# Band attention in a two-layer encoder: softmax weights of seven head pairs turned by VectorE and a DRAM round trip

## What is computed

```python
sc = jnp.einsum('bqhd,bkhd->bhqk', qc, kc).astype(jnp.float32) * scale + bias[None]
sc = jnp.where(valid[None, None, None, :], sc, NEG_INF)
p = jax.nn.softmax(sc, axis=-1).astype(vc.dtype)
return jnp.einsum('bhqk,bkhd->bqhd', p, vc)
```

## Time and profile before

| | |
|---|---|
| median of 3 runs | 1094.41 us (1094.17 to 1094.53) |
| profiled execution, own time | 1094.57 us |
| its span in the trace | 1092.8 us |
| mean granted clock of TensorE | 0.999 of full speed |
| TensorE matmul busy | 1085.8 us |
| VectorE, ScalarE, GpSimd busy | 642.3, 469.5, 521.3 us |
| DMA | 106 GB/s over the span |

### The profile page before, as it was taken

How to read it: one execution, slowest core, us unless ns; L and a number is a source line. 1 busy time by engine, 2 the same in 40 slices (tenths; PEclk the granted TensorE clock), 3 DMA queues, 4 the chain that set the end, 5 groups by cost and what they waited for, 6 DMA issues and landing times.

```text
span 1092.8 us, 15012 instructions
## 1 busy us (share of the span) xinstructions
PE 1085.8 (99%) x5040; PEld 902.6 (83%) x5040; DVE 642.3 (59%) x1081; ACT 469.5 (43%) x698; POOL 521.3 (48%) x408
## 2 busy tenths in 40 slices
PE   9999999999999999999999999999999999999998
PEld 7888888888888888888888888888888888888886
DVE  6586557766666642223488777766777676751103
ACT  7874443433333333323555555564443333333213
POOL 6578635544444545554433333344544444445541
PEclk9999999999999999999999999999999999999999
DMA  9382323222222233333322222222322222224312
GB/s 307 98 261 97 116 78 111 101 96 96 96 96 96 97 101 111 110 101 115 116 87 89 97 81 97 75 77 78 116 96 96 96 96 96 96 97 139 114 36 77
DMA packets 44726, 115.63 MB, mean 106 GB/s; under 512 B 11376, under 2 KB 13552, under 8 KB 44688
## 3 DMA queue, kind: packets, MB, share of 16 engines
q1 hardware_dynamic: 42224, 110.65, 30.7%
q10 hardware_dynamic: 2464, 4.47, 1.3%
HBM read 111.92 MB, written 6.59 MB: 108 GB/s over the span
## 4 chain that ended last, share of the span: by engine, by line
PE 99%; DMA 0%; ACT 0%; DVE 0%; SPq 0%; issue 0%; DVEq 0%; ACTq 0%
PE bank L1493 29%; PE bank L1495 29%; PE bank L1494 28%; PE bank L1580 2%; PE bank L1781 2%; PE bank L1778 2%; PE bank L1780 2%; PE bank L1955 2%; PE bank L1940 2%; PE bank L1970 1%; PE bank L1969 1%; DMA x<-x_in 0%; PE bank L1756 0%; PE bank L1755 0%; DVE rows_out L1466 0%; ACT xh L567 0%
## 5 line engine op out<-in xcount | busy, mean ns | idle before, releaser
L472 POOL TENSOR_TENSOR wl<-raw,wh 128x512 fp32r<-128x512 f32 x187 | 244.7, 1309 | 540.9 <-ACT wh L563 540.9
L563 ACT ACTIVATE wh<-raw 128x1024 fp32r<-128x1024 f32 x187 | 197.7, 1059 | 354.7 <-PE bank L1495 284.0
L1493 PE MATMUL bank<-xh,wh 128*128 128x512 f32 x880 | 344.5, 392 | 0.0
L1495 PE MATMUL bank<-xh,wl 128*128 128x512 f32 x880 | 342.9, 390 | 0.0
L1494 PE MATMUL bank<-xl,wh 128*128 128x512 f32 x880 | 342.8, 390 | 0.0
L474 POOL TENSOR_TENSOR wl<-raw,wh 128x512 fp32r<-128x512 f32 x187 | 253.8, 1357 | 0.0
L1493 PEld LDWEIGHTS bank<-xh,wh 128*128 128x128 f32 x880 | 165.3, 188 | 34.5
L1495 PEld LDWEIGHTS bank<-xh,wl 128*128 128x128 f32 x880 | 165.2, 188 | 34.5
L1494 PEld LDWEIGHTS bank<-xl,wh 128*128 128x128 f32 x880 | 165.4, 188 | 33.6
L1494 PE MATMUL bank<-al,wh 128*128 128x512 f32 x252 | 98.1, 389 | 0.0
L1493 PE MATMUL bank<-ah,wh 128*128 128x512 f32 x252 | 98.1, 389 | 0.0
(11 more groups left out here) (245 smaller groups left out, 1480.5 us busy)
## 6 DMA issues: line engine op xcount, KB each, us to landing
raw<-weights SPq DMA_DIRECT2D x187, 512.0 KB, 3.3
bias_scratch<-ext_scratch SPq DMA_DIRECT2D x1, 4096.0 KB, 17.9
bias<-bias_scratch ACTq DMA_DIRECT2D x8, 512.0 KB, 3.5
raw<-weights SPq DMA_DIRECT2D x8, 256.0 KB, 7.3
x<-x_in SPq DMA_DIRECT2D x8, 256.0 KB, 7.0
out<-rows_out SPq DMA_DIRECT2D x4, 256.0 KB, 2.0
x_rows<-blocks SPq DMA_DIRECT2D x16, 48.0 KB, 2.6
out<-x SPq DMA_DIRECT2D x3, 256.0 KB, 2.6
```

What stands on the lines that cost most here:

```text
L472: nc.gpsimd.tensor_tensor(low[:, 0:FIRST], raw[:, c % RAW, 0:FIRST], high[:, 0:FIRST], ALU.subtract).then_inc(w_half, 1)
L563: nc.scalar.activation(wh[:, c % RING].rearrange("p k c -> p (k c)"), raw[:, c % RAW], ACT.Copy).then_inc(w_hi, 1)
L1493: nc.tensor.matmul(dst, w_hi_part, m_hi, start=first, stop=False)
L1495: return nc.tensor.matmul(dst, w_lo_part, m_hi, start=False, stop=last)
```

## The change

P of the pairs 0 to 6 is no longer turned by TensorE. ScalarE normalises P in place (`normalise` moved from VectorE); VectorE turns each of the ten 128 x 128 blocks of a head within its 32 x 32 blocks (`turn_p`, 20 instructions a pair) into `p_blocks`; SyncE stores each head's 640 KB to a DRAM scratch `p_scratch` (of shape 2 x 128 x 1280) and, when that has landed, loads it back with four DMAs of 32 partitions each, which bring the 32 x 32 blocks to their places, into `pt`. `pt` shares its memory with `ptl`, `p_blocks1` with `p_sb`. ScalarE writes the high part from `pt`, two instructions a head, GpSimd the low part. `weighted_v(c - 1)` runs in pair c: inside K of the next pair, and in the pairs 4 and 5 behind it. It reads P and writes PSUM in pieces of 32 columns. The low part of Q moves from VectorE to GpSimd. The first part of Q of the pair after takes five of eight steps, not four. The output halves of the first pairs' result move one pair back, so that pair 4 has none, and two more fall into the last pair. Pair 7 still turns P on TensorE (`transpose_p`, `weighted_v_last`), between other products. Banks, waits, unit numbers and the packing order of the weights follow; SyncE's loop over the weight units is written out around the attention, since the stores and loads of P stand between its loads. Below is the diff's core, with the indentation cut.

```diff
-Q_AHEAD = KT // 2
+Q_AHEAD = 5
+AV_AFTER_K = (4, 5)
 EARLY = PAIRS // 2
...
+TURNED_AT = [0, 4, 7, 9]
+QUARTER = P_COLS // 4
+FIRST_UNROLLED, LAST_UNROLLED = 15 * RAW, 22 * RAW
...
+ptl_at = nc.sbuf_base
 ptl = att_mem("ptl", [P, 2, P_COLS], F32R)
+pt = nc.alloc_sbuf_tensor_at("pt", [P, 2, P_COLS], F32, offset=ptl_at)
...
+p_blocks = [att_mem("p_blocks0", [P, 4, QUARTER], F32),
+            nc.alloc_sbuf_tensor_at("p_blocks1", [P, 4, QUARTER], F32, offset=p_sb_at)]
...
+def first_unit(c):
+    return U_PAIR + 3 * c - (c > EARLY)
+def split_unit(c):
+    return U_PAIR + 3 * c + 3 - (c > EARLY)
...
+def store_blocks(c, hh):
+    sp.wait_ge(p_turned, 10 * (2 * c + hh) + 10)
+    sp.wait_ge(p_in[hh], 64 * c)
+    sp.dma_start(p_d[hh], p_blocks[hh][:].rearrange("p b n -> p (b n)")).then_inc(p_stored[hh], 16)
+def load_turned(c, hh):
+    sp.wait_ge(p_stored[hh], 16 * c + 16)
+    sp.wait_ge(av_mm, 2 * c)
+    for b in range(4):
+        sp.dma_start(pt[32 * b:32 * b + 32, hh].rearrange("p (a n) -> p a n", a=4),
+                     bass.AP(p_d.tensor, hh * P * P_COLS + b * QUARTER,
+                             [[P_COLS, 32], [32 * P_COLS, 4], [1, QUARTER]])).then_inc(p_in[hh], 16)
+with sp.Fori(0, FIRST_UNROLLED // RAW - 3) as turn:
+    for c in range(3 * RAW, 4 * RAW):
+        load_unit(c, turn)
+n = FIRST_UNROLLED
+for c in range(PAIRS - 1):
+    while n < first_unit(c + 1) + RAW:
+        load_unit(n)
+        n += 1
+    store_blocks(c, 0)
+    store_blocks(c, 1)
+    load_turned(c, 0)
+    load_turned(c, 1)
+for c in range(n, LAST_UNROLLED):
...
+def p_split_lo(c, hh):
+    for n in range(2):
+        pool.wait_ge(p_hi, 4 * c + 2 * hh + n + 1)
+        at = slice(2 * QUARTER * n, 2 * QUARTER * n + 2 * QUARTER)
+        nc.gpsimd.tensor_tensor(ptl[:, hh, at], pt[:, hh, at], pth[:, hh, at], ALU.subtract).then_inc(p_lo, 1)
+def q_split_lo(c):
+    pool.wait_ge(qk_hi, 2 * c + 1)
+    nc.gpsimd.tensor_tensor(ql[:], q_sb[:], qh[:], ALU.subtract).then_inc(ql_pool, 1)
+for c in range(FIRST_UNROLLED, U_PAIR + 3):
+    split_lo(c)
+for c in range(PAIRS - 1):
+    unit = split_unit(c)
+    q_split_lo(c + 1)
+    split_lo(unit)
+    split_lo(unit + 1)
+    p_split_lo(c, 0)
+    if c != EARLY and c != PAIRS - 2:
+        split_lo(unit + 2)
...
+def normalise(c, hh):
+    act.wait_ge(rsum_inv, 2 * c + hh + 1)
+    for h, i in SCORE_STEPS:
+        if h == hh:
+            blk = p_sb[:, hh, P_OFF[i]:P_OFF[i] + P * (i + 1)]
+            nc.scalar.activation(blk, blk, ACT.Copy, scale=psums[:, 4 * hh + i:4 * hh + i + 1]
+                                 ).then_inc(p_norm, 1)
+def p_split_hi(c, hh):
+    act.wait_ge(p_in[hh], 64 * c + 64)
+    if c:
+        act.wait_ge(av_mm, 2 * c)
+    for n in range(2):
+        at = slice(2 * QUARTER * n, 2 * QUARTER * n + 2 * QUARTER)
+        nc.scalar.activation(pth[:, hh, at], pt[:, hh, at], ACT.Copy).then_inc(p_hi, 1)
 def attend(c):
-    following = c < PAIRS - 1
-    unit = U_PAIR + 3 * (c + 1)
-    if following:
-        load_bias(c + 1)
-    exponentials(c)
+    unit = split_unit(c)
+    load_bias(c + 1)
+    exponentials(c, 0)
+    normalise(c, 0)
+    exponentials(c, 1)
+    normalise(c, 1)
+    split_qk(c + 1, 0)
     split_hi(unit)
-    if following:
-        split_qk(c + 1, 0)
-    for t in range(TR_EACH):
+    if c in AV_AFTER_K:
+        split_hi(unit + 1)
+        split_qk(c + 1, 1)
+        if c == EARLY:
+            for n in range(4):
+                split_second_v(n)
+    if c:
+        half_o(c - 1, 0)
+        half_o(c - 1, 1)
+    if c not in AV_AFTER_K:
+        split_hi(unit + 1)
+    if c:
+        split_o(c - 1)
+    if c not in AV_AFTER_K:
+        split_qk(c + 1, 1)
+    p_split_hi(c, 0)
+    if c != EARLY and c != PAIRS - 2:
+        split_hi(unit + 2)
+    p_split_hi(c, 1)
+    if c == PAIRS - 2:
+        split_hi(unit + 2)
+def attend_last(c):
+    unit = split_unit(c)
+    for hh in range(2):
+        exponentials(c, hh)
+        normalise(c, hh)
+    half_o(c - 1, 0)
+    half_o(c - 1, 1)
+    split_transposed(c, 0)
+    split_o(c - 1)
+    split_hi(unit)
+    for t in range(1, TR_EACH):
         split_transposed(c, t)
     split_hi(unit + 1)
-    if c == EARLY - 1:
-        for n in range(4):
-            split_second_v(n)
-    if following:
-        split_qk(c + 1, 1)
     half_o(c, 0)
     half_o(c, 1)
     split_o(c)
     split_hi(unit + 2)
+    split_hi(unit + 3)
...
-        dve.wait_ge(qk_lo, 2 * c + which - 1)
+        if which == 0 and c > 1:
+            dve.wait_ge(ql_pool, c - 1)
+        else:
...
-            dve.wait_ge(ptr_mm, TR_EACH * c)
+        if c:
+            dve.wait_ge(p_stored[1], 16 * c)
...
+def inverse_sums(c, hh):
     dve.wait_ge(exp_done, 8 * c + 4 * hh + 4)
     r = psums[:, 4 * hh:4 * hh + 4]
     nc.vector.reciprocal(r, r).then_inc(rsum_inv, 1)
-    dve.wait_ge(rsum_inv, 2 * c + hh + 1)
-    for h, i in SCORE_STEPS:
-        if h == hh:
-            blk = p_sb[:, hh, P_OFF[i]:P_OFF[i] + P * (i + 1)]
-            ts(blk, blk, psums[:, 4 * hh + i:4 * hh + i + 1], None, ALU.mult).then_inc(p_norm, 1)
+def turn_p(c, hh):
+    dve.wait_ge(p_norm, 8 * c + 4 * hh + 4)
+    if c:
+        dve.wait_ge(p_stored[hh], 16 * c)
+    if hh:
+        dve.wait_ge(p_turned, 10 * (2 * c + hh))
+    for i in range(4):
+        for j in range(i + 1):
+            at = 32 * (TURNED_AT[j] + i - j)
+            blk = p_sb[:, hh, P_OFF[i] + P * j:P_OFF[i] + P * j + P].rearrange("p (b c) -> p b c", b=4)
+            nc.vector.transpose(p_blocks[hh][:, :, at:at + 32], blk).then_inc(p_turned, 1)
...
+def all_scores(c):
+    for g in range(3):
+        scores(c, g, 0)
+    scores(c, 0, 1)
+    inverse_sums(c, 0)
+    scores(c, 1, 1)
+    scores(c, 2, 1)
 def attend(c):
-    following = c < PAIRS - 1
-    if not following:
+    all_scores(c)
+    qk_evacuate(c + 1, 0)
+    inverse_sums(c, 1)
+    if c < EARLY:
         vw_evacuate(c, 0)
-    for hh in range(2):
-        for g in range(3):
-            scores(c, g, hh)
-    normalise(c, 0)
-    if following:
-        qk_evacuate(c + 1, 0)
-        vw_evacuate(c, 0)
-    normalise(c, 1)
+    if c == EARLY + 1:
+        second_v_lo(2)
+        second_v_lo(3)
+    turn_p(c, 0)
+    if c == EARLY:
+        qk_evacuate(c + 1, 1)
+    turn_p(c, 1)
     if c < EARLY:
         vw_evacuate(c, 2)
+        vw_evacuate(c, 1)
+        vw_evacuate(c, 3)
+    elif c > EARLY:
+        vw_evacuate(c - 1, 0)
+        vw_evacuate(c - 1, 1)
+    if c in AV_AFTER_K:
+        if c > EARLY:
+            qk_evacuate(c + 1, 1)
+        qk_split_lo(c + 1, 1)
+        if c == EARLY:
+            second_v_lo(0)
+    if c:
+        o_add(c - 1, 0)
+        o_add(c - 1, 1)
+    if c not in AV_AFTER_K:
+        qk_evacuate(c + 1, 1)
+    if c and c != PAIRS - 2:
+        o_split_lo(c - 1)
     if c == EARLY:
-        second_v_lo(2)
+        second_v_lo(1)
+    if c not in AV_AFTER_K:
+        qk_split_lo(c + 1, 1)
+    if c == PAIRS - 2:
+        o_split_lo(c - 1)
+def attend_last(c):
+    vw_evacuate(PAIRS - 2, 0)
+    all_scores(c)
+    inverse_sums(c, 1)
+    vw_evacuate(PAIRS - 2, 1)
+    o_add(c - 1, 0)
+    o_add(c - 1, 1)
     transposed_split_lo(c, 0)
-    if following:
-        qk_split_lo(c + 1, 0)
-    for t in range(1, TR_EACH):
+    o_split_lo(c - 1)
+    for t in range(1, 3):
         transposed_split_lo(c, t)
-    vw_evacuate(c, 1)
-    if c < EARLY:
-        vw_evacuate(c, 3)
-    if c == EARLY - 1:
-        second_v_lo(0)
-        second_v_lo(1)
-    if c == EARLY:
-        second_v_lo(3)
-    if following:
-        qk_evacuate(c + 1, 1)
-        qk_split_lo(c + 1, 1)
+    vw_evacuate(PAIRS - 1, 0)
+    for t in range(3, TR_EACH):
+        transposed_split_lo(c, t)
+    vw_evacuate(PAIRS - 1, 1)
     o_add(c, 0)
     o_add(c, 1)
...
-        pe.wait_ge(score_out, 8 * c + 8)
-    else:
-        pe.wait_ge(vw_out, vw_count(c, 0))
+    if n:
+        pe.wait_ge(score_out, 8 * c + [4, 5, 8][n - 1])
...
-    pe.wait_ge(qk_lo, 2 * c + 2)
+    pe.wait_ge(qk_lo, c + 2)
     if c == 0:
         pe.wait_ge(v_lo_done, 4)
     for g in range(3):
-        if g != 1 and c >= 1:
-            pe.wait_ge(o_sum, 2 * c - 1 + g // 2)
+        if g < 2 and 2 <= c <= EARLY:
+            pe.wait_ge(o_sum, 2 * c - 3 + g)
+        if g == 1 and c > EARLY:
+            pe.wait_ge(o_sum, 2 * c - 2)
+        if g == 0 and c >= 1:
+            pe.wait_ge(ql_pool, c)
+            pe.wait_ge(vw_out, 4 * c if c <= EARLY else 4 * EARLY + 2 * (c - EARLY - 1))
         for n, (i, col) in enumerate(SCORE_GROUPS[g]):
             keys = P * (i + 1)
...
     pe.wait_ge(v_lo_done, 4 if c < EARLY else 8)
-    pe.wait_ge(ptr_lo, TR_EACH * (c + 1))
+    pe.wait_ge(p_lo, 4 * c + 4)
     for hh in range(2):
-        if hh:
-            pe.wait_ge(vw_out, vw_count(c, 1))
+        pe.wait_ge(score_out, 8 * c + 9 + 2 * hh if c < EARLY - 1 else 8 * c + 16)
+        dst = bank[av_bank(c, hh)][:].rearrange("p (i a t) -> p a i t", i=4, a=4)
+        for j in range(4):
```

(75 more changed lines are left out.)

58 lines of the change are left out of this document (37 added, 21 removed).

## The result

The changed kernel takes **1097.76 us** (median of 8 runs, 1097.04 to 1098.66) against 1094.53 (8 runs, 1094.17 to 1094.84) before: a ratio of 1.0031, 95% interval 1.002 to 1.0042. It is slower by 3.2 us. The forecast was 1088.0, faster than before; the result is slower than before and lies just above the top of the range, 1097. The profiled execution took 1097.62.

A forecast was written before the change was run, and what follows sets the result against it. TensorE, busy 1085.8 of 1092.8 us, was taken as the bound. From 1094.57, a gain of 15.3 less 8.75 of waits left 6.6, forecasting 1088.0 us; the range was 1081 to 1097.

The forecast's parts named there:

- The gain: TensorE loses the transposes of P, 2.18 us in each of seven pairs: 15.3 us saved.
- C: Rival: products with V take longer in pieces of 32 columns; at twice the time, 17.4 us more, 1105; chance 0.05.
- The turning: VectorE's 20 instructions a pair on 128 x 128 blocks of P: 0.22 us each, 4.4 us.
- the 12.0 us up to the last turned block: From ScalarE's first exponential through the second reciprocal (6.98), a V tile (0.65) and the turning (4.4): 12.0 us.
- The shape of the ring: ScalarE's first exponential to the next pair's: 12.0 to turned blocks, 7.9 store and load, 1.3 high part: 21.2 us.
- pair 5's scores for the result: Pair 5's scores on TensorE wait for the last addition of the result, late after short pair 4: 3.15 us.
- pair 7's products for the score groups: In pair 7, pair 6's products with V wait until all scores are in SBUF, behind VectorE's reciprocal: 1.75 us.
- The 1.85 before pair 7's transposes: In pair 7, TensorE's transposes of head 1 wait for its scaling: 1.85 us.
- D: Rival: nothing comes late and every wait is covered, 1079.3 us; chance 0.05.
- store and load, 3.95 each, 7.9 together: P's trip through DRAM: 640 KB store, then load, scaled from the 512 KB weight load; bounds 2.0 to 6.5 each.
- beside the transfer: The four loads of P are issued on SyncE at about 0.33 us each, overlapping the transfer, costed at nothing.
- B: Rival: ring longer than 21.2 us, delaying ScalarE in every pair; 7 us per us of ring, loss from 22.1; chance 0.23.

The follow-up runs named there:

- the version with both deferred: Changed kernel with both heads' high parts of P written in the next pair and GpSimd's third weight unit split before P: 1091.76 us, ratio 0.9976.
- The experiment on VectorE's order: Changed kernel with VectorE taking the last two score groups of head 1 before head 0's reciprocal: 1099.6 us, ratio 1.0046.
- the kernel without the trip: Changed kernel without the stores and loads of P, the high part taken from the memory of P's low part: 1081.21 us, ratio 0.9882.
- the fastest version: Four stores and one load a head, both high parts deferred, plus pair 3's result ahead in pair 4 and pair 6's head 0 split early: 1090.18 us.
- the version with both edits together: Changed kernel with four stores and one load a head, and both high parts of P written in the next pair: 1090.56 us, ratio 0.9966.

## Why the prediction was wrong

**Right.** The gain: 15.3 us, by full pairs of 21.24 and a short one of 15.80 without the trip. The products with V cost what they did, 2.49 us for 16 at full clock; C is rejected. The turning, 0.21 us apart where 0.22 was taken, and the 12.0 us up to the last turned block (11.6). The shape of the ring, what stands in it, and two of the waits behind it: pair 5's scores for the result, 1.83 where 3.15 was forecast, and pair 7's products for the score groups, 1.98 where 1.75 was. The 1.85 before pair 7's transposes did not come. D is rejected.

**The step that failed is the term "store and load, 3.95 each, 7.9 together", with the four issues put "beside the transfer".** It measures 10.2 in pair 1 and 9.2 to 9.8 in pairs 3 to 6, by three pieces:
- The issues are in series with the transfers. The last load can't start before the ones ahead of it are issued, at 0.43 each and 0.47 apart, not 0.33: three behind head 1's store, 1.3 us, and 3.2 in pair 1, where head 0's four stand there too. The prediction's 0.33 is the length of an issue by itself. I had the wrong end of it: with four loads, what counts is the landing of the last.
- The last load lands in 4.3 to 5.6 instead of 3.95, with two heads' P under way; with one head alone it is 2.9 to 4.0. B named "both heads' transfers at once", but the term was priced with one.
- The stores are better than I took: 3.3 in the median, 2.9 alone.

For one head the sum of 7.9 fits (7.8 to 8.7 measured), but by luck: the store that was priced too high makes up for the issues that were priced at nothing.

The rest follows from it. B priced the ring at 7 us per us above 21.2; the measured mean of 22.67 gives 1088.0 + 7 x 1.47 = 1098.3, and 1097.76 was measured. The 7 us are seven rings one behind the other, and the same line fits the other kernels that leave the reader in the ring: 1118.5 for a ring of 25.55 (eight loads; 1118.07 measured) and 1087.5 for 21.13 (one head; 1087.0). So the step from ring to time held, though its constant is partly luck: the late start of 0.9 and the half clock in pair 7, 1.65, were not in it, and the 1.85 before pair 7's transposes was. The chances did not hold: 0.45 on a ring within half a us of a pair's length, with a term for which no row existed, was too much. The bounds of that term, 4.0 to 13.0, were wider by far than the range that I made of them.

The Trainium skill, DMA: Bandwidth & Descriptors (section Anatomy of one DMA), gives a formula fitted on DMAs that GpSimd issues, and by it an estimate of 3.5 for 640 KB. SyncE's store takes 2.9 by itself in six pairs of seven (3.8 in pair 1), so the measurement decides; for a second DMA beside it the formula has no term. The rule of the Trainium skill, VectorE: DVE Perf Modes (Rules for kernel authors), 128 x 128 transposes to TensorE, came out right in sign for this kernel; by the version with both deferred it is the reader's place that decides, not the route.

**Missed, and found by the profile.** The bank of V's fourth tile (0.8 to 1.5 us in pairs 1 to 3); I had walked VectorE's list for K and the result and not for the banks that its scores free. The experiment on VectorE's order shows that it is how the ring shows itself there, not a cost of its own. And the half clock, below, about 1.6 us in pair 5 and 1.65 in pair 7.

**Left open.** The attention starts at 538.82 in the changed kernel against 537.90 before, at 538.2 to 538.8 in all experiments; 0.3 to 0.9 us of the result lie ahead of the pairs, and no run tells why. Why pair 1's first store takes 4.9 us, and 3.8 with one head alone, is open too. Pair 7's waits behind GpSimd's low parts could be tried against by giving half of them to VectorE; that was not done.

## What to carry over

A round trip through DRAM is priced as store, issues and load in series, each with all that is under way beside it, and by the last DMA of a set, not the first. If its reader sits in an engine's list where the next round starts, its length sets the pace of the whole loop; moved to where it has a whole round's time, it costs next to nothing, as the full pairs of 21.25 to 21.4 show with the same bytes and a trip of up to 12.9 us. The short and last rounds, where TensorE has nothing to put in between, then become the bound, and there waits only move until an engine's list gets shorter.

## What the runs showed of the hardware

TensorE's clock falls after a wait in this kernel. Behind the 1.83 us before pair 5's scores, the profile after has:

```profile
648.88 0.71 PE L1673 MATMUL bank<-xh,wh 128*128 128x512 f32 x1
649.39 0.63 PE L1674 MATMUL bank<-xl,wh 128*128 128x512 f32 x1
649.82 0.63 PE L1675 MATMUL bank<-xh,wl 128*128 128x512 f32 x1
...
652.38 0.41 PE L1675 MATMUL bank<-xh,wl 128*128 128x512 f32 x1
652.63 0.40 PE L1673 MATMUL bank<-vo,wh 128*128 128x512 f32 x1
```

Eight matmuls start 0.43 us apart, twice the 0.227 of the earlier trace rows, so at the lower level, 1.2 GHz; then the pitch is back at 0.23 to 0.25. The granted clock of the stretch is 0.93. It starts 1.4 us after the wait's end, and the eight cost 8 x 0.2 = 1.6 us, nearly as much as the wait. In pair 7 the products with V, behind 1.98 us of wait, take 4.13 us instead of 2.49. So a wait of about 1.8 cost 3.4. The length of a wait alone doesn't tell: in the kernel without the trip the 1.08 us at the same place in pair 5 have nothing behind them (granted clock 1.00), and neither have 1.66 us in the fastest version, 2.09 in the one with the store in four pieces nor 3.05 in the one with eight loads, while 1.74 and 4.24 in the version with both edits together and 3.97 in the one with eight loads have. What decides was not tried.

A store of 640 KB lands in 2.9 us in six of seven pairs when it travels alone, and head 1's in 3.3 to 3.5 in six of seven beside head 0's transfers; pair 1's takes 3.8 and 4.2. The last 160 KB piece of the load lands in 2.9 to 4.0 alone and, in pairs 1 to 6, in 4.3 to 5.6 beside the other head's.

An issue right behind another keeps SyncE longer than one by itself, for weight loads and loads of P alike. A weight load by itself in the changed kernel, and two behind the four loads of pair 2 in the one that sends one head's P:

```profile
565.18 0.33 SPq L419 DMA_DIRECT2D raw<-weights  x1
```

```profile
597.20 2.64 SPq L468 DMA_DIRECT2D pt<-p_scratch  x4
599.88 0.90 SPq L419 DMA_DIRECT2D raw<-weights  x2
```

In the changed kernel the first load of a set takes 0.30 to 0.33 and the ones straight behind it 0.43 in the median; 169 weight loads by themselves have a median of 0.33, and 26 straight behind another DMA 0.43. So it isn't the pattern of the load that costs the 0.1 us, but its place in a row of issues.

GpSimd subtracts 640 columns in 1.57 us, 2.5 ns a column, as for 512.
